# Input product of the short convolution: seven half-sized products for eight

## The reference

```python
def short_conv_mixer(h, w_in, conv_w, w_out):
    gate_b, gate_c, v = jnp.split(h @ w_in, 3, axis=-1)
    return (gate_b * dwconv_centred(gate_c * v, conv_w)) @ w_out
```

## Time and profile before

| | us |
|---|---|
| median of 3 runs | 3531.86 (3530.76 to 3533.32) |
| the profiled execution, its own time | 3532.93 |
| its span | 3531.1 |
| PE busy | 3348.5 (95%) |
| DVE busy | 1931.3 (55%) |
| ACT busy | 1378.3 (39%) |
| POOL busy | 559.9 (16%) |
| mean granted clock of PE | 0.976 |

### The profile page before, as it was taken

The page is one execution under the profiler, slowest core; times in us unless marked ns, Lnnn a source line. Parts: engine busy times, 40 slices in busy tenths (PEclk is TensorE's granted clock), DMA queues, the critical chain, the costliest instruction groups (busy, mean ns, idle before and its releaser), DMA issues. The chain is left out here.

```text
span 3531.1 us, 75240 instructions
## 1 busy us (share of the span) xinstructions
PE 3348.5 (95%) x31534; PEld 2871.7 (81%) x31534; DVE 1931.3 (55%) x3276; ACT 1378.3 (39%) x1973; POOL 559.9 (16%) x792
## 2 busy tenths in 40 slices
PE   7999999999799998989999989959999999999997
PEld 5778888787677877878888878849999999999997
DVE  4666766667445655762212236666656665666563
ACT  5445454444255655330000013424444444444442
POOL 3555545564100000000000000000000100010000
PEclk9999999999899999999999999959999999999999
DMA  4221222211233434331111135426666666666662
GB/s 144 56 83 50 71 68 68 77 50 44 65 126 125 138 126 138 133 94 30 50 39 30 49 107 173 160 95 226 203 217 211 203 203 215 213 202 205 212 214 72
DMA packets 361219, 439.96 MB, mean 125 GB/s; under 512 B 15236, under 2 KB 300196, under 8 KB 360100
## 3 DMA queue, kind: packets, MB, share of 16 engines
q1 hardware_dynamic: 351784, 403.20, 35.3%
q0 software_dynamic: 9216, 33.56, 4.1%
HBM read 369.59 MB, written 67.13 MB: 124 GB/s over the span
## 5 line engine op out<-in xcount | busy, mean ns | idle before, releaser
L2655 PE MATMUL bank<-ex_x_hi,ex_w_lo 128*128 128x256 f32 x2048 | 581.4, 284 | 2.0 <-DVE ex_x_lo L2837 2.0
L2656 PE MATMUL bank<-ex_x_lo,ex_w_hi 128*128 128x256 f32 x2048 | 580.2, 283 | 0.0
L2657 PE MATMUL bank<-ex_x_hi,ex_w_hi 128*128 128x256 f32 x2048 | 580.1, 283 | 0.0
L2651 DVE TENSOR_TENSOR ex_w_lo<-ex_w_loaded,ex_w_hi 128x2048 fp32r<-128x2048 f32 x192 | 434.0, 2289 | 226.9 <-ACT ex_w_hi L2647 222.5
L2647 ACT ACTIVATE ex_w_hi<-ex_w_loaded 128x2048 fp32r<-128x2048 f32 x192 | 359.4, 1905 | 173.3 <-PE bank L2657 169.3
L2655 PEld LDWEIGHTS bank<-ex_x_hi,ex_w_lo 128*128 128x128 f32 x2048 | 393.6, 192 | 2.8 <-issue 2.2
L2656 PEld LDWEIGHTS bank<-ex_x_lo,ex_w_hi 128*128 128x128 f32 x2048 | 393.7, 192 | 0.6
L2657 PEld LDWEIGHTS bank<-ex_x_hi,ex_w_hi 128*128 128x128 f32 x2048 | 393.7, 192 | 0.0
L2711 POOL CAST ex_idx<-moe_idx_all 128x2 uint32 (+1 forms) x16 | 3.0, 186 | 1777.6 <-POOLq L79 1466.3
L264 PE MATMUL bank<-columns_columns_hi,weights_weights_lo 128*128 128x512 f32 x544 | 226.9, 417 | 8.9 <-DVE columns_columns_lo L848 3.8
L2811 ACT ACTIVATE ex_hid_hi<-ex_hidden 128x256 fp32r<-128x256 f32 x128 | 53.4, 417 | 414.0 <-DVE ex_hidden L2860 414.0
(11 more groups left out here) (474 smaller groups left out, 8265.4 us busy)
## 6 DMA issues: line engine op xcount, KB each, us to landing
ex_w_loaded<-in_wg SPq DMA_DIRECT2D x64, 1024.0 KB, 5.3
ex_w_loaded<-in_wu SPq DMA_DIRECT2D x64, 1024.0 KB, 6.8
ex_w_loaded<-in_wd SPq DMA_DIRECT2D x64, 1024.0 KB, 5.0
plain_weights<-in_w_in SPq DMA_DIRECT2D x70, 512.0 KB, 4.7
gl_ada_tile<-in_ada_w SPq DMA_DIRECT2D x48, 512.0 KB, 4.3
plain_columns<-hT_dram SPq DMA_DIRECT2D x14, 1024.0 KB, 7.4
sc_w_loaded<-in_sc_w_in SPq DMA_DIRECT2D x23, 512.0 KB, 6.5
plain_columns<-in_x SPq DMA_DIRECT2D x16, 512.0 KB, 5.5
```

Of the source, the lines that this page charges most:

```text
L2651: nc.vector.tensor_tensor(w_lo[c % SPLIT][:], raw[:, c % LOADED, :], w_hi[c % SPLIT][:].bitcast(F32), ALU.subtract).then_inc(s["lo"], 1)
L2655: nc.tensor.matmul(psum, ll, rh, start=first, stop=False)
L2656: nc.tensor.matmul(psum, lh, rl, start=False, stop=False)
L2657: return nc.tensor.matmul(psum, lh, rh, start=False, stop=last)
```

## The change

`out_product` no longer splits the first 512 tokens and the first weights ahead, and no longer makes the first quarter of the next stage's product. In its steps 10 to 13 DVE makes sums over the first 1024 tokens instead (`differences`). In its second use it now loads all its weights itself. `each_step` unrolls four more steps.

`short_conv` is written anew. It works in 24 units: two groups of 1024 tokens, four pairs of 128-feature blocks, three weight tiles (i = 0 gate_c, 1 v, 2 gate_b). A unit multiplies a 256-feature, 1024-row weight tile by 1024 tokens. Both are cut in 2 x 2 parts, and the four output parts are made of seven products of sums (A.. and S.. of weights, B.. and T.. of tokens), each 4 x 3 = 12 matmuls, into four banks of PSUM (`BANK_OF`). The three last products of a unit are added onto banks whose content must have been read before (semaphores p1 and c22). The other engines now have these parts:

- SP loads 1 MB of weights per unit into a single buffer (`raw`), and after each third unit stores 1 MB, in one queue in the order of the loop below.
- ACT makes 7 high parts of weights per unit (128 x 512 each), keeps product 0 (`keep_p1`), and at the start and at the switch of groups makes 7 high parts of tokens (128 x 2048 each).
- DVE makes 4 weight sums and 7 low parts per unit (128 x 512), adds the products together (`middle`, `corner`, `rest`), convolves in every third unit (`convolve`, two rows of 1025), and at the switch makes 4 token sums and 7 low parts (128 x 2048 each).

The core of the diff (the sums and low parts follow the pattern shown; S1, S3, S2, S4 and T1, T3, T2, T4 are their orders):

```diff
# each_step
-    for a, b in ((2, EARLY // 2 + 1), (EARLY // 2 + 1, TT // 2 - 1)):
+    for a, b in ((2, EARLY // 2 + 1), (EARLY // 2 + 1, TT // 2 - 3)):
...
-    for t in range(TT - 2, TT + 3):
+    for t in range(TT - 6, TT + 3):
# Ahead
+        self.w_raw = sb(nc, ctx, "first_w", [P, KD, 2 * P])
# out_product, SP, second use
+                    for c in range(2):
+                        sp.dma_start(raw[c], wv[quarter(c)]).then_inc(loaded[c], 16)
+                        if c == 0:
+                            sp.dma_start(mt[0][:], mv[:, :, at(0)]).then_inc(m_in[0], 16)
# out_product, PE, first use
-                        ahead.passes(nc, bank[q][:], ahead.w_hi, ahead.w_lo, q)
# out_product, DVE, first use
+                def differences(n):
...
+                    dve.wait_ge(s["kept"], 16)
+                    nc.vector.tensor_tensor(t1, b12, b11, ALU.subtract).then_inc(s["differences"], 1)
+                    dve.wait_ge(s["differences"], 3 * n + 1)
+                    nc.vector.tensor_tensor(b12, b22, b12, ALU.subtract).then_inc(s["differences"], 1)
+                    nc.vector.tensor_tensor(t2, b22, t1, ALU.subtract).then_inc(s["differences"], 1)
...
-                            if early[0] and is_tile(t - 2):
...
+                            if isinstance(t, int) and TT - 6 <= t < TT - 2:
+                                differences(t - TT + 6)
# short_conv
+    UNITS = GROUPS * PAIRS * 3
+    A11, S1, S3, S2, A12, A22, S4 = range(7)
+    B11, T1, T3, T2, B21, T4, B22 = range(7)
+    BANK_OF = (0, 3, 2, 1, 0, 2, 3)
+    LO_ORDER = (A11, S3, S1, S2, A12, A22, S4)
# SP
+                def store(n):
+                    g, c, _ = parts(n)
+                    sp.wait_ge(s["ended"], n + 1)
...
+                for n in range(1, UNITS + 1):
+                    if n < UNITS:
+                        _, c, i = parts(n)
+                        sp.wait_ge(s["w_lo"], 7 * n - 1)
+                        sp.dma_start(raw[:], wv[:, :, AT[i] + c * 2 * P:AT[i] + (c + 1) * 2 * P]).then_inc(s["raw"], 16)
+                    if n % 3 == 0:
+                        store(n - 1)
# PE, product at of unit n
+                        pe.wait_ge(s["t_lo"], 7 * g + at + 1)
+                        pe.wait_ge(s["w_lo"], 7 * n + LO_ORDER.index(at) + 1)
...
+                        if at == 4:
+                            pe.wait_ge(s["p1"], n + 1)
+                        if at >= 5:
+                            pe.wait_ge(s["c22"], 2 * n + at - 4)
...
+                        for kb in range(H):
+                            nc.tensor.matmul(psum, w_lo[:, at, kb, :], hi[:, kb, :], start=(kb == 0 and not more), stop=False, skip_group_check=more)
+                            nc.tensor.matmul(psum, w_hi[:, at, kb, :], lo[:, kb, :], start=False, stop=False, skip_group_check=more)
+                            mm = nc.tensor.matmul(psum, w_hi[:, at, kb, :], hi[:, kb, :], start=False, stop=(kb == H - 1), skip_group_check=more)
+                        mm.then_inc(s["u"], 1)
# ACT: a high part waits for raw, for its sum, and for PE to be done with the old one
+                        wait_for(act, s["raw"], 16 * n)
# DVE (go: issue, then wait until it is done)
+                def middle(n):
+                    dve.wait_ge(s["u"], 7 * n + 4)
+                    dve.wait_ge(s["p1"], n + 1)
+                    go(nc.vector.tensor_tensor(um[:], um[:], x(n, 1)[:], ALU.add))
...
+                    go(nc.vector.tensor_tensor(part, um[:], x(n, 2)[:], ALU.add), s["c22"])
+                    go(nc.vector.tensor_tensor(part, part, x(n, 3)[:], ALU.add), s["c22"])
+                    if not first:
+                        save_u(n, 1)
+                        go(nc.vector.tensor_tensor(dst, dst, tmp[:], ALU.mult))
...
+                for n in range(UNITS):
+                    switch, more, i = n == UNITS // 2 - 1, n + 1 < UNITS, n % 3
+                    def ahead_of_middle():
+                        weights_lo(n + 1, A11)
+                        weights_sum(n + 1, S1)
+                        weights_sum(n + 1, S3)
+                        weights_lo(n + 1, S3)
+                    if n == 0:
+                        middle(0)
+                    weights_lo(n, S4)
...
+                    if n:
+                        rest(n - 1, 0, 3, s["ended"])
...
+                    if i == 2:
+                        convolve(n)
+                    if switch:
+                        turned_sum(1, T1)
+                        turned_sum(1, T3)
+                    if more and i < 2:
+                        ahead_of_middle()
+                    if n:
+                        middle(n)
+                    if more and i == 2:
+                        ahead_of_middle()
...
+                        weights_sum(n + 1, S2)
+                        weights_sum(n + 1, S4)
+                        weights_lo(n + 1, S1)
...
+                        weights_lo(n + 1, S2)
...
+                    corner(n)
...
+                        weights_lo(n + 1, A12)
+                    rest(n, 1, 2)
...
+                        weights_lo(n + 1, A22)
# DVE, at the switch of groups (n = 11 and 12), between the above:
#   n = 11: turned_sum T1, T3 | middle | turned_lo B11 | turned_sum T2 | turned_lo T1, T3 | ... | turned_sum T4
#   n = 12: weights_lo S4 | turned_lo T2 | rest(11, 0) | turned_lo B21, T4, B22 | ahead_of_middle | middle(12)
```

More of the change, by code:

```diff
@@ L1890, in __init__, with out_product @@
         F32R = mybir.dt.float32r
-        shapes = [("hT", [P, KD, T]), ("first_w", [P, KD, P])]
+        shapes = [("hT", [P, KD, T]), ("differences", [P, 2, KD // 2, 512])]
         with Phase("plain") as plain:
[L1893 to L1912, removed]
+            self.plain, self.diff = [sb(nc, plain, n, shape) for n, shape in shapes]
+        self.lo, self.diff_lo = [sb(nc, ctx, f"{n}_split", shape, F32R) for n, shape in shapes]
+        self.w_raw = sb(nc, ctx, "first_w", [P, KD, 2 * P])
+        self.w_next = w_in.rearrange("(kb p) n -> p kb n", p=P)[:, :, D:D + 2 * P]
+def out_product(nc, k, mT, w, resid, gate_row, norm_row, scale_row, shift_row, store, turn_dst, g_col, cols_dram, final, ahead=None, cols_buf=None):
     first = final is not None
@@ L2243, in short_conv @@
         cw = sb(nc, ctx, "conv_cols", [P, KD * 3])
-        w_next = w_out.rearrange("(kb p) n -> p kb n", p=P)
-        gv = sb(nc, ctx, "gated", [P, T + 2])
-        acc = sb(nc, ctx, "conv", [P, T])
+        last_gv = sb(nc, ctx, "last_gated", [P, PAIRS, 2, 2])
+        last_u = sb(nc, ctx, "last_u", [P, PAIRS, 2])
         bank = k.bank
[L2248 to L2262, removed]
+        raw = ahead.w_raw
+        def parts(n):
+            return n // (3 * PAIRS), n // 3 % PAIRS, n % 3
@@ new lines, in of_tokens, with tokens, tokens_lo @@
+        def of_tokens(both, diff, fourth, g, piece):
+            a = g * HALF
+            where = {B11: (0, a), T3: (0, a + QT), B21: (H, a), B22: (H, a + QT)}
+            if piece in where:
+                kb, at = where[piece]
+                return both[:, kb:kb + H, at:at + QT]
+            return fourth[:] if piece == T4 else diff[:, 0 if piece == T1 else 1, :, :]
+        def tokens(g, piece):
+            return of_tokens(ahead.plain, ahead.diff, t4, g, piece)
+        def tokens_lo(g, piece):
+            return of_tokens(ahead.lo, ahead.diff_lo, t4_lo, g, piece)
@@ L2264, in short_conv, with a_raw, sum_of, x @@
+        def a_raw(piece):
+            kb, f = {A11: (0, 0), A12: (H, 0), A22: (H, P)}[piece]
+            return raw[:, kb:kb + H, f:f + P]
+        def sum_of(piece):
+            return s4_raw if piece == S4 else w_sum[:, piece]
+        a21 = raw[:, 0:H, P:2 * P]
+        def x(n, m):
+            return bank[4 * (n % 2) + m]
         with nc.Block() as block:
@@ L2374, in short_conv @@
+                rest(UNITS - 1, 0, 3, s["ended"])
         meet(nc, s)
```

328 lines of the change are left out of this document (204 added, 124 removed).

## The result

The changed kernel takes 3566.52 us (median of 4, 3564.27 to 3567.77) beside 3532.43 us (4, 3530.76 to 3533.32) for the kernel before on the same chip: a ratio of 1.0093, 95% interval 1.0081 to 1.0105, so 34 us slower. The prediction said 3569 (3543 to 3592). The profiled execution has 3567.28 us, its span 3565.5, 34.4 more than before.

The account below looks back on a forecast made before the run. PE, busy 95% of the span, was taken as the bound. Stage +27.5, `differences` +1.1, last store +3.4 and second out_product +4.6 made +36.6 us on the profiled 3532.9: 3569.5, stated as 3569 (3543 to 3592).

Parts of the forecast that it names:

- products, 2016 x 0.2268: PE in the convolution stage: seven products for eight, 457.2 us of matmuls in place of 517.1, 59.9 less.
- lead-in: Start of the convolution stage: PE waits for B11's low part, there at +5.7 us.
- The stall: PE idle before product 5 after each gate_b unit, via store, load and DVE: 6.9 us, six times (first 7.3), 41.6.
- The pair of DMAs: SP's queue: a 1 MB load issued 0.4 behind a store lands 8.8 us after the store's issue (5.3 to 10.3).
- Rival A: The load does not queue behind the store and lands 5.3 us after the store's issue: 3545.5 us; chance 0.17.
- Rival D: PE: products of 12 matmuls restart more often; 168 product boundaries cost at most 4 us, 1.5 more than now.
- The switch: Token groups change in units 11 and 12: PE 31.1 us idle in five pieces, including unit 12's stall (24 to 36).
- The clock behind the stalls: PE's low clock: 2.0 us behind each of six stalls and the switch's last, 14 in all (0 to 20).
- The start: Units 0 and 1 of the stage: PE loses 5.2 us between products, 2.0 to low clock, 2.3 for unit 1's load.
- The lead into the stage: First out_product: `differences` makes the DVE chain that ends the stage about 1.1 us late (0 to 3).
- The neighbours behind: After the stage: last 1 MB store +3.4 us (2 to 5), second out_product loading its own weights +4.6 (3 to 8).
- Rival B: DVE and the load keep ahead of PE in every third unit: seven stalls and their clock go, 3507 us; chance 0.07.

Follow-up runs that it names:

- run 1: Changed kernel with SP issuing each load ahead of the store, without waiting for the old unit's end: 3522.68 us, 0.997 of the kernel before.
- run 3: Changed kernel with `middle` ahead of the next load's pieces on DVE in gate_c units too: 3520.79 us, 0.9965 of the kernel before.
- run 2: Changed kernel with the load ahead of the store, but still waiting for the old unit's end: 3552.99 us, 1.0055 of the kernel before.
- run 5: Changed kernel with 24 unused matmuls ahead of product 5 of each gate_c unit but the first: 3552.96 us, 1.0054 of the kernel before.
- run 9: Changed kernel without `differences`, T1 and T2 of the first group read from B12 and B21: 3567.70 us, 1.0093 of the kernel before.
- run 4: Changed kernel with the load ahead of the store without its wait, and `middle` ahead of the next weights: 3510.69 us, 0.9937 of the kernel before.
- run 6: Run 4 with the four token sums of the switch made by GpSimd in place of DVE: 3512.73 us, 0.9936 of the kernel before.
- run 8: Run 6 with GpSimd's sums held until the convolution of unit 11 has ended: 3510.73 us, 0.9927 of the kernel before.

## Why the prediction held, step by step

For the stage, the starts of all 2016 matmuls were read from the timeline in a row; a start over 0.24 us behind the last one counts as slow, one with an idle time in its row as a wait.

| term (us) | predicted | measured |
|---|---|---|
| products, 2016 x 0.2268 | 457.2 | 457.2 |
| lead-in | 5.7 | 5.7 |
| waits of unit 0, and of unit 1 | 5.2 + 2.3 | 4.4 + 2.0 |
| six stalls, units 3, 6, 9, 15, 18, 21 | 41.6 | 39.6 |
| switch, five waits | 31.1 | 22.0 |
| low clock: lead-in; behind the seven stalls; inside the switch; small | 2.0; 14; in the row above; 0 | 1.5; 15.1; 6.7; 0.8 |
| rest (an idle time is counted from a matmul's end, 0.16 behind its due successor: 16 of them) | 0.2 | 2.7 |
| stage | 559.3 | 557.9 |

- **The stall** is right in place and cause, and nearly in size: product 5 of units 3, 6, 9, 15, 18 and 21, 6.3 to 7.2 us each, 39.6 where 41.6 stood. Its links were 8.1 for the load behind the store (predicted 8.4), and 5.5 from the load to PE's restart (1648.23 to 1653.78, predicted 5.5). Runs 1 and 3 each take away one link and with it all but 1.0 to 2.3 us, so DVE did not lack time in sum.
- **The pair of DMAs**: the price came from two loads, and the forecast that a load and a store queue in the same way was right for this order (there 8.5 after the store's issue, 8.8 predicted). Rival A, 5.3, was wrong. But it is sharing rather than queueing: in run 2 the load that goes first is slowed too. The prediction says that no row of a store followed by a load decides between the two. The trace of the kernel before has one:

```profile
2024.35 0.37 SPq L2273 DMA_DIRECT2D z_dram<-sc_conv  x1
2024.93 0.38 SPq L2280 DMA_DIRECT2D next_w<-in_sc_w_out  x1
```

Both are 1 MB, the load in pieces of 2 KB instead of 1 KB and with another load 1.3 behind it. The store landed 5.0 after its issue, and the load 7.2 after its own, which is 7.8 after the store's. This row speaks against A. (At 7.2 it is also dearer than the 6.6 that the prediction takes for the dearest 1 MB load.)
- **Rival D**: the starts add up to the stage's 557.9 with every term named, so product boundaries cost nothing that can be seen.
- **The switch** was mis-sized by 2.4 us, not by the 9.1 between the two idle times. The 31.1 were time at full clock, with the low clock inside the switch "hidden in the next wait", and this holds. From one token wait's end to the next took 9.65, 13.23 and 15.53 us in the changed kernel, with 1.4, 2.6 and 2.7 us of slow matmuls in them. In run 5 it took 9.65, 13.23 and 15.43, with 0, 1.4 and 1.6 (two of the rows below), and in run 9 9.65, 13.23 and 15.52, with 0, 3.0 and 1.6. DVE sets these times, and slow matmuls only fill what would be idle. So the 22.0 and the 6.7 belong together: 28.7 where 31.1 stood.

```profile
1838.08 0.79 PE L2325 MATMUL bank<-sc_tokens_hi,sc_w_lo 128*128 128x512 f32 x1 [6.64 <-DVE hidden_differences_split L2418]
...
1851.31 0.79 PE L2325 MATMUL bank<-sc_tokens_hi,sc_w_lo 128*128 128x512 f32 x1 [6.17 <-DVE hidden_differences_split L2418]
```

- **The clock behind the stalls**: 14 predicted, 15.1 by the distances (13.2 behind the six and 1.9 in unit 12), 13.6 by run 5.
- **The start** is 1.6 under, 0.5 of it clock. (The prediction calls its 545.3 a sum at full clock, but 2.0 of low clock at the lead-in are in it.)
- **The lead into the stage** (a): 1.1 predicted for `differences`, 0.72 by run 9. The other 2.3 of the 3.0 were not predicted. 1.8 of them are there before the first `differences`: PE turns its tiles 11.77 us apart in both kernels, 1.8 later in the changed one from the first steps on. Executions of the changed kernel's first stages differ by more than that (the keeping of tile 1 starts at 1397.98 in run 5 and at 1405.06 in run 2), so one profile of each kernel can't put this down to the change. The last 0.45 are the last eight transposes: 1.94 us at 1.2 GHz behind 7.79 us of idle time, instead of 1.07, so that DVE stands 1.27 for them instead of 0.82. Before, PE worked on the next stage's first quarter there and stood 2.83. That the missing matmuls let the clock fall was not tried by itself.
- **The neighbours behind**: the last store +2.8 (predicted 3.4: its landing takes 4.3, not 4.9), the second out_product's start +3.7 (predicted 4.6: the weights are there after 5.2, not 6.0).
- **The closeness of the sum** is part luck. Stalls, switch, start and the neighbours behind came out 2.0, 2.4, 1.6 and 1.5 shorter than predicted; the lead into the stage, the clock behind the stalls, the small low-clock stretches and the rest 1.9, 1.1, 0.8 and 2.5 longer, and what follows 1.2 shorter.
- **Rival B**, faster, was priced at 3507 for a DVE and a load that keep ahead. Run 4, which builds just that, gives 3510.7. So the arithmetic is worth 22 us even in this schedule, and two orders of issue cost 56.

The Trainium skill's page "TensorE: Matmul & The Clock Gate", section "Loop structure matters more than you think", has a PE that waits for a DMA between matmuls fall to the low clock. Here PE waits for DVE, which waits for the DMA. Run 5 agrees, with 13.6 us, and so does run 4, with a stage clock of 0.97 against 0.93.

## What to carry to other kernels

A change that takes work from the bounding engine is paid by the queues that it lengthens: write out for one unit of the loop when each in-order queue (SP's too) reaches each instruction, and compare that with the due time. A mean load of 14.7 in 19.05 us said "fits" here, and the order of two DMAs and of two groups of DVE instructions decided between 0.9% slower and 0.6% faster. A load never goes behind a store that waits for compute, and work on a critical bank goes ahead of preparation that may wait for memory.

## What the runs showed of the hardware

- Here DVE instructions with both operands in SBUF stood while a GpSimd subtraction over 128x2048 in SBUF ran, until it ended: 4.98 and 9.90 us where 0.69 and 1.29 are normal (1.29: the pair of L2393 in the changed kernel), 17.75 for 4.87; those with one operand in PSUM did not (0.69). I had costed GpSimd as a free engine. The Trainium skill's page "SBUF — State Buffer", section "Who interferes with whom", says so: the two share a pair of ports, held for a whole instruction, and an instruction of DVE with two SBUF inputs contends with a GpSimd one that reads SBUF. The traces agree.
- A GpSimd subtraction over 128x2048 took 4.6 to 5.3 us where DVE's took 2.29.
- A 1 MB load took 5.1 to 5.7 us with a 1 MB store issued 2.0 us behind it, 6.5 to 6.6 with the store 0.4 behind it, and 7.8 to 8.6 with the store 0.4 ahead.
- Behind the same idle time of 7.54 us, in the same code, PE's low clock cost 1.5 us in the changed kernel's profile and in those of runs 2 and 6, and 2.9 to 3.1 in those of runs 1, 3, 4, 5 and 8. A single profile prices a stretch of low clock to no better than that.
